# GpSimd or VectorE for the long levels' operands in a gated linear recurrence beside a GEMM

## The reference, cut to what matters

```python
    bcum = jnp.cumsum(log_g..., axis=3)
    diff = bcum[..., :, None, :] - bcum[..., None, :, :]
    decay = jnp.where(causal, jnp.exp(jnp.where(causal, diff, 0.0)), 0.0)
    scores = jnp.einsum('bhnid,bhnjd,bhnijd->bhnij', qf, kf, decay)
    o_intra = jnp.einsum('bhnij,bhnjv->bhniv', scores, vf)
    ...
    o_inter = jnp.einsum('bhncd,nbhdv->bhncv', qf * jnp.exp(bcum), states_prev)
    return (o_intra + o_inter).reshape(b_, h_, s_, dv)
```

## Time and profile before

| | |
|---|---|
| median of 3 runs | 2396.09 us (2396.05 to 2398.22) |
| the profiled execution | 2396.95 us, span 2395.2 us |
| busy over the span | PE 2337.4 us (98%), DVE 1314.2 (55%), ACT 911.5 (38%), POOL 780.2 (33%) |
| the recurrence | from about 329 to 776 us of the span |

### The profile page before, as it was taken

One profiled execution on the slowest core, in us unless ns is written; L12 is line 12 of the kernel. 1 busy time (PEld: TensorE's weight loads), 2 busy tenths in 40 slices (PEclk: granted clock), 3 DMA queues, 4 the chain that ended last, 5 costly groups with the idle time before them and its releaser, 6 DMA issues.

```text
span 2395.2 us, 39157 instructions
## 1 busy us (share of the span) xinstructions
PE 2337.4 (98%) x15544; PEld 2049.8 (86%) x15544; DVE 1314.2 (55%) x2648; ACT 911.5 (38%) x1678; POOL 780.2 (33%) x705
## 2 busy tenths in 40 slices
PE   8999999999999999999999999999999999999998
PEld 7889978798888899999888899888899888887798
DVE  4003269999997433271232655456455455577536
ACT  5124654444444432232222333333333334455320
POOL 3121334445654221222443343243243242232112
PEclk9999999999999999999999999999999999999999
DMA  6234334343334422132333524314324314475621
GB/s 245 96 121 163 139 130 151 124 142 115 115 128 165 175 97 80 53 124 102 110 106 117 184 72 150 115 71 150 115 71 150 115 71 181 142 266 185 222 86 71
DMA packets 139053, 312.23 MB, mean 130 GB/s; under 512 B 12288, under 2 KB 55936, under 8 KB 127616
## 3 DMA queue, kind: packets, MB, share of 16 engines
q1 hardware_dynamic: 80192, 223.85, 27.5%
q10 hardware_dynamic: 58688, 86.00, 9.9%
HBM read 211.77 MB, written 98.04 MB: 129 GB/s over the span
## 4 chain that ended last, share of the span: by engine, by line
PE 88%; DVE 8%; issue 1%; ACT 1%; DMA 1%; POOL 0%; DVEq 0%; ACTq 0%; SPq 0%
PE bank L410 12%; PE bank L412 12%; PE bank L411 12%; PE bank L421 9%; PE bank L422 8%; PE bank L423 8%; PE bank L2486 3%; PE bank L2509 3%; PE bank L1853 3%; PE bank L1851 3%; PE bank L1852 3%; PE bank L1470 1%; PE bank L2475 1%; PE bank L734 1%; PE bank L2791 1%
## 5 line engine op out<-in xcount | busy, mean ns | idle before, releaser
L410 PE MATMUL bank<-at_hi,w_hi 128*128 128x512 f32 x1408 | 581.7, 413 | 2.3 <-DVE stage L2017 0.9
L412 PE MATMUL bank<-at_hi,w_lo 128*128 128x512 f32 x1408 | 552.3, 392 | 0.0
L411 PE MATMUL bank<-at_lo,w_hi 128*128 128x512 f32 x1408 | 550.9, 391 | 0.0
L421 PE MATMUL bank<-w_hi,at_hi 128*128 128x256 f32 x1792 | 520.7, 291 | 0.8 <-issue 0.8
L376 POOL TENSOR_TENSOR w_lo<-w_raw,w_hi 128x2048 fp32r<-128x2048 f32 x69 | 318.4, 4614 | 594.6 <-ACT w_hi L389 570.5
L423 PE MATMUL bank<-w_hi,at_lo 128*128 128x256 f32 x1792 | 508.4, 284 | 0.0
L422 PE MATMUL bank<-w_lo,at_hi 128*128 128x256 f32 x1792 | 508.4, 284 | 0.0
L421 PEld LDWEIGHTS bank<-w_hi,at_hi 128*128 128x128 f32 x1792 | 345.3, 193 | 7.4 <-issue 5.6
L422 PEld LDWEIGHTS bank<-w_lo,at_hi 128*128 128x128 f32 x1792 | 344.9, 192 | 0.8 <-issue 0.2
L423 PEld LDWEIGHTS bank<-w_hi,at_lo 128*128 128x128 f32 x1792 | 344.5, 192 | 0.0
L410 PEld LDWEIGHTS bank<-at_hi,w_hi 128*128 128x128 f32 x1408 | 268.4, 191 | 64.1 <-issue 11.7
(11 more groups left out here) (313 smaller groups left out, 3849.8 us busy)
## 6 DMA issues: line engine op xcount, KB each, us to landing
w_raw<-in_weights SPq DMA_DIRECT2D x84, 1024.0 KB, 7.4
feat<-stage ACTq DMA_DIRECT2D x184, 256.0 KB, 2.0
tok<-stage ACTq DMA_DIRECT2D x72, 256.0 KB, 2.2
stage<-feat SPq DMA_DIRECT2D x32, 256.0 KB, 3.6
w_mem<-in_w_mem SPq DMA_DIRECT2D x4, 1024.0 KB, 5.8
x<-in_x SPq DMA_DIRECT2D x4, 1024.0 KB, 11.8
logg<-gate_g ACTq DMA_DIRECT2D x8, 512.0 KB, 3.0
rec_b<-logg SPq DMA_DIRECT2D x16, 256.0 KB, 5.6
```

The costliest lines, as they stand in the source:

```text
L410: nc.tensor.matmul(ps_gemm[i % 2], wh, ah, start=(k == 0), stop=False)
L411: nc.tensor.matmul(ps_gemm[i % 2], wh, al, start=False, stop=False)
L412: last = nc.tensor.matmul(ps_gemm[i % 2], wl, ah, start=False, stop=(k == KT - 1))
L421: nc.tensor.matmul(o, ah, wh, start=(k == 0), stop=False)
```

## The change

VectorE makes the operands of the four long levels, two levels (four products) at the end of each chunk, in a new function `long_operands`; in even chunks it first waits for what GpSimd waited for. In the second of the two chunks its last product raises `r_Z`. GpSimd's list keeps the roots alone. `level_operands` becomes a form of `operand_levels`, which takes a range of levels. `operands` stays for `first_pool`. The rest, with DMAs and queues, is as it was.

```diff
+        def long_operands(dve, head, mixer, u, part):
+
+            here = unit_tokens(u)
+            if part == 0:
+                dve.wait_ge(r_in_qk[u // 2], head * 32 + 32)
+                dve.wait_ge(r_E, head * 16 + (4 * u + 1))
+            last = operand_levels(dve, u, here, range(FIRST // 2 * part, FIRST // 2 * (part + 1)))
+            if part == 1:
+                last.then_inc(r_Z, 1)
+
...
         def level_operands(eng, u, here, part):
 
-            for j in part_levels(part):
+            return operand_levels(eng, u, here, part_levels(part))
+
+        def operand_levels(eng, u, here, levels):
+
+            for j in levels:
...
         def head_pool_rec(pool, head, mixer, after):
             for c in range(NT):
-                if c % 2 == 0 and (after or c + 4 < 2 * UNITS):
-                    operands(pool, *ahead(head, mixer, after, c + 4)[:3])
                 pool.wait_ge(r_ss, head * 8 + (c + 1))
...
                 if then:
                     rec_place(dve, *then)
+                pair = c // 2 * 2
+                if after or pair + 4 < 2 * UNITS:
+                    long_operands(dve, *ahead(head, mixer, after, pair + 4)[:3], c % 2)
                 if head or c:
                     for n in rec_tiles_of(head - (c == 0), (c - 1) % NT):
                         low_after(dve, n)
```

## The result

The changed kernel takes 2402.82 us (median of 16 runs, 2400.33 to 2407.03) against 2397.67 us for the kernel before, timed beside it (16 runs, 2394.71 to 2403.80). The ratio is 1.0022, with a 95% interval of 1.0015 to 1.0028: slower by 0.22%, about 5.3 us. The profiled execution took 2401.83 us, its span 2400.0.

What follows compares the result with a forecast made beforehand. It took TensorE and VectorE as both nearly full, VectorE the fuller in heads 4 and 6. Added: +4 us of load and +2.4 for one clock fall, +6.4 on 2396.95, 2403.4; as median 2402.5 us, range 2396 to 2409.

Steps and rivals of the forecast that it cites:

- VectorE as the bound of heads 4 and 6: Heads 4 and 6: VectorE already the fuller engine, its need after the change 55.1 and 55.2 us.
- +4 us without the clock: Recurrence: growth before any clock fall, 2.2 + 1.5 + 0.5, about +4 us.
- my sum: Heads 1 to 6: larger of TensorE's and VectorE's needs added, 334.5 us, plus 1.5 for the misfit.
- one fall of 2.4 us: Ends of heads 4 and 6: one clock fall counted of one to two expected, 12 matmuls at half pace, +2.4 us.
- Rival A: Heads' ends: no fall of the clock, the rest as forecast, +3 to +4.8 us, 2399 to 2400.9; chance 0.25.
- Three to 3.5 us in one piece: Ends of heads 4 and 6: TensorE's idle time stands there as a single stall of 3 to 3.5 us.
- The relief: VectorE in the recurrence: 38 us given back once GpSimd's 240 products are gone, bounds 24 and 44.
- the net load: VectorE: +48 - 38 = +10 us in the recurrence, 6.5 - 4.8 = +1.7 us per head.
- Rival B: Recurrence: several clock falls and GpSimd's roots starved, ScalarE's normed result late; +8 to +14 us, 2404 to 2410; chance 0.20.
- Rival C: Recurrence: faster, relief worth more and new products fill only holes, 2390.6 us; chance 0.12.
- Rival D: Recurrence: VectorE's +10 us hidden in its 31 idle ones, 2396 us; chance 0.08.

Runs made afterwards that it cites:

- w4: Changed kernel plus three 128x256 matmuls of constants on TensorE in the wait at the end of heads 0 to 6; 2399.66 us, ratio 1.0003 to the kernel before.
- w3: Changed kernel with chunk 7's four products moved behind the head's last two gated results; 2399.11 us, ratio 1.0000 to the kernel before.
- x3: w3, but GpSimd makes levels 0 and 1 and VectorE levels 2 and 3, one a chunk; 2392.68 us, ratio 0.9978 to the kernel before.
- w1: Changed kernel with seven of a unit's eight long-level products made on neither engine; 2385.99 us, ratio 0.9949 to the kernel before.
- w2: Changed kernel with one level a chunk on VectorE instead of two, levels 2 and 3 left out; 2389.58 us, ratio 0.9960 to the kernel before.
- x4: Kernel before with the scores' place scaling on ScalarE, at heads' ends behind the normed result; 2393.97 us, ratio 0.9992.

## Why the prediction was right, and where it wasn't

**Right in the main, with some luck in the number.** Forecast 2402.5 us and slower, measured 2402.8. That the two meet within 0.3 us is luck: I added 6.4 us to a median of three runs, 2396.1, which was 2397.7 over sixteen, and the growth was 5.2 us. VectorE as the bound of heads 4 and 6: in five kernels that share head 4's matmuls, its length follows VectorE's busy time nearly one for one once this is above TensorE's. +4 us without the clock: two profiles without a fall in the recurrence behind its start, before and w4, take 434.0 and 438.4 us for it, 4.4 more; heads 1 to 6 take 336.1 us in w4, and my sum gave 334.5 + 1.5. By the medians w4 is only 0.8 us over the kernel before (-1.4 to +2.9 by its interval). That is less than 4 us, but the kernel before ran at a lower mean clock there, 0.9941 against 0.9956, so it spent some 7 us more at 0.50, an estimate of 3 us at what w4's falls cost. The 4 us aren't confirmed to better than about 2.

**The clock.** I counted one fall of 2.4 us behind heads 4 or 6, of one to two. Rival A, no fall, is out for the profiled execution: there were two, worth 1.6 and 2.8 us by TensorE's busy time, but one came behind head 0, after a stall of 2.04 us, which I had put under what it takes. The Trainium skill (TensorE: Matmul & The Clock Gate, "What's actually happening") says that TensorE has its full rate only while it is kept busy, which w4 bears out. Whether a given stall ends in a fall can't be read from its length: 2.08 us behind 0.97 did it ahead of head 5 and not ahead of head 7, and in w3 1.27 behind 0.98 did it.

**The stall's shape.** "Three to 3.5 us in one piece" was wrong: at the ends of heads 4 and 6 TensorE stands twice, 0.97 us for the gated result of chunk 5 and 2.08 for that of chunk 6, with one turn between. The sum, 3.05, was right. Heads 1 to 3 stayed within 1 us, head 1 just (0.96 more, with a fall that cost 1.6). Head 5 was to take 51 to 52.5 us and took 55.1; without the fall, in w4, 52.6, so its excess was the clock, which I hadn't put there.

**The relief.** 38 us was its size, and 33 its worth: with GpSimd's operands gone 4.3 us over the quiet steps remain, 2.7 of them at the sums over levels, which I had booked on GpSimd. VectorE's busy time was to be 427 us and is 431.9, which is this difference. Nor was the net load the same +1.7 us in every head: heads 2, 4 and 6, with two `low_after`, got 1.3, 1.2 and 0.9 us of busy time more in w4, heads 1, 3 and 5 got 2.5, 2.3 and 3.4. I took GpSimd's operands as 0.16 us each, whatever their number, and x3 shows that this is false below eight in a burst.

**Rival B, the starved roots.** The chain did grow: the powers' mean on GpSimd rose from 936 to 1193 ns, and one lasts 6.92 us at 537.61, 6.11 before. It is kept out by some twenty VectorE instructions in a row, not by one.

```profile
537.61 6.92 POOL L301 TENSOR_TENSOR small<-small,cols 128x1 f32<-128x1 f32 x1
```

But no matmul of TensorE waited for ScalarE's normed result; the stalls name VectorE, and the weight loads' waits for that result went down, from 8.3 to 5.3 us. This part of B didn't happen. **Rival C** fell with w1: relief alone is worth 12 us, and holes for the new products there weren't. **Rival D** fell with the knee in w2: half of the products are nearly hidden, all of them aren't.

## What to carry to other kernels

Two engines at 96% and 93% of a stretch are two bounds: put each one's need beside the other's, stage by stage, and an added microsecond costs little up to the crossing (2.8 us for the first half of the products here) and nearly a full one beyond it in a head that this engine bounds. It is a first cut, since head 5 of x4 is longer than both needs. Moving work off GpSimd gives back what its instructions cost VectorE, here 33 us, but count what VectorE then does itself, here 48 (240 steps of 0.20 us); a split of the work can beat both ends, as in x3. A stall of 2 us or so on TensorE may cost as much again in matmuls at half clock, so look at the granted clock behind each stall, and put whatever nobody waits for behind the instruction that releases TensorE.

## What I had not expected of the hardware

Half of GpSimd's operands cost VectorE a quarter of what all of them did (8 us for 33). A GpSimd instruction of 4.6 us held a VectorE instruction with one tile and a column of scalars as its inputs, 4.28 us instead of 0.25, so that 12 of them took 45 us from VectorE. The other way round, VectorE's instructions in a row kept a power of 0.55 us on GpSimd for 6.92 us. And the clock fell once after a stall of 2.04 us and once after 0.98 and 1.27, while the pair of 0.97 and 2.08 us brought it down in one head and not two heads later.
